# Sums of the queries' squares in the second layer: four-column weights over 512 moving columns, one bank for all pairs, one turn at the end

## The reference, cut to what matters

```python
q = (rms_norm(q_lat, q_a_norm) @ w_uq).reshape(B, S, MLA_HEADS, MLA_QK_DIM)   # 8 heads, 192 = 128 + 64
...
q = rms_norm(q, q_head_norm)          # over the 192 numbers of each token and head
k = rms_norm(k, k_head_norm)
...
q = jnp.concatenate([q[..., :MLA_NOPE_DIM], rope(q[..., MLA_NOPE_DIM:], pos)], axis=-1)
...
o = causal_softmax_attention(q, k, v, 1.0 / math.sqrt(MLA_QK_DIM)).reshape(B, S, MLA_WIDTH)
```

## Time and profile before

| | us |
|---|---|
| median of 3 runs | 1964.53 (1963.85 to 1965.43) |
| the profiled execution | 1966.32, its span 1963.5 |
| TensorE busy | 1875.1, 95% of the span |
| VectorE, ScalarE, GpSimd busy | 966.9, 794.5, 466.8 |
| granted TensorE clock, mean | 0.977 of full |

### The profile page before, as it was taken

One profiled execution on the slowest core, in us unless ns is written; L12 is line 12 of the kernel. 1 busy time (PEld: TensorE's weight loads), 2 busy tenths in 40 slices (PEclk: granted clock), 3 DMA queues, 4 the chain that ended last, 5 costly groups with the idle time before them and its releaser, 6 DMA issues.

```text
span 1963.5 us, 24681 instructions
## 1 busy us (share of the span) xinstructions
PE 1875.1 (95%) x9738; PEld 1481.7 (75%) x9742; DVE 966.9 (49%) x1575; ACT 794.5 (40%) x1401; POOL 466.8 (24%) x471
## 2 busy tenths in 40 slices
PE   6999998999999989999999999999998999999997
PEld 5987776777677756667888888877877788888885
DVE  5345554575446678744433333454555353333334
ACT  4235663444435355554441323233444334232322
POOL 0035541101312124541120201005555202010200
PEclk9999999999999989999999999999999899999999
DMA  4321111221012410001332223221111023223231
GB/s 153 95 78 51 44 43 54 75 86 54 1 53 84 125 54 22 23 23 55 95 98 97 97 86 103 91 86 59 60 54 55 23 85 108 97 94 99 88 100 71
DMA packets 40289, 143.32 MB, mean 73 GB/s; under 512 B 4592, under 2 KB 4976, under 8 KB 40176
## 3 DMA queue, kind: packets, MB, share of 16 engines
q1 hardware_dynamic: 40176, 141.76, 22.5%
HBM read 139.64 MB, written 2.10 MB: 72 GB/s over the span
## 4 chain that ended last, share of the span: by engine, by line
PE 86%; DVE 5%; ACT 4%; POOL 2%; issue 2%; DMA 0%; DVEq 0%; SPq 0%; ACTq 0%; POOLq 0%
PE BANK L273 22%; PE BANK L274 22%; PE BANK L275 22%; PE BANK L854 2%; PE BANK L627 2%; PE BANK L1596 2%; PE BANK L1553 1%; PE BANK L1577 1%; PE BANK L612 1%; PE BANK L911 1%; DVE LH L717 1%; ACT WH L250 1%; PE BANK L2335 1%; PE BANK L2282 1%; PE BANK L2322 1%
## 5 line engine op out<-in xcount | busy, mean ns | idle before, releaser
L250 ACT ACTIVATE WH<-WRAW 128x1024 fp32r<-128x1024 f32 x262 | 273.6, 1046 | 486.6 <-PE BANK L275 449.5
L259 DVE TENSOR_TENSOR WL<-WRAW,WH 128x1024 fp32r<-128x1024 f32 (+1 forms) x249 | 324.8, 1305 | 269.1 <-ACT WH L250 267.6
L273 PE MATMUL BANK<-HH,WH 128*128 128x512 f32 x1048 | 428.5, 409 | 18.6 <-DVE WL L259 18.0
L274 PE MATMUL BANK<-HH,WL 128*128 128x512 f32 x1048 | 411.1, 392 | 0.0
L275 PE MATMUL BANK<-HL,WH 128*128 128x512 f32 x1048 | 410.9, 392 | 0.0
L273 PEld LDWEIGHTS BANK<-HH,WH 128*128 128x128 f32 x1048 | 199.1, 190 | 69.9 <-ACT WH L250 18.7
L274 PEld LDWEIGHTS BANK<-HH,WL 128*128 128x128 f32 x1048 | 198.7, 190 | 44.0 <-issue 5.9
L275 PEld LDWEIGHTS BANK<-HL,WH 128*128 128x128 f32 x1048 | 198.3, 189 | 42.6
L2223 POOL TENSOR_TENSOR HID<-TMP,HID 128x512 fp32r<-128x512 f32 x64 | 83.1, 1299 | 532.9 <-ACT HID L2204 532.9
L273 PE MATMUL BANK<-HID,WH 128*128 128x512 f32 x512 | 203.0, 396 | 0.0
L274 PE MATMUL BANK<-HID,WL 128*128 128x512 f32 x512 | 203.0, 396 | 0.0
(11 more groups left out here) (383 smaller groups left out, 3169.9 us busy)
## 6 DMA issues: line engine op xcount, KB each, us to landing
WRAW<-in_w SPq DMA_DIRECT2D x77, 512.0 KB, 3.5
WRAW<-in_wu SPq DMA_DIRECT2D x64, 512.0 KB, 3.3
WRAW<-in_wd SPq DMA_DIRECT2D x64, 512.0 KB, 3.3
WRAW<-in_w0o SPq DMA_DIRECT2D x8, 512.0 KB, 3.4
WRAW<-in_w1o SPq DMA_DIRECT2D x8, 512.0 KB, 3.5
WRAW<-in_wc SPq DMA_DIRECT2D x8, 512.0 KB, 3.3
WRAW<-in_w2o SPq DMA_DIRECT2D x8, 512.0 KB, 3.4
WRAW<-in_w3o SPq DMA_DIRECT2D x8, 512.0 KB, 3.2
```

What stands on the lines that cost most here:

```text
L250: e.activation(WH[b % NS][:, 0:n], WRAW[b % NR][:, 0:n], ACT.Copy).then_inc(*inc("s_high", ("high", b)))
L259: e.tensor_tensor(WL[b % NS][:, 0:n], WRAW[b % NR][:, 0:n], WH[b % NS][:, 0:n].bitcast(F32), ALU.subtract).then_inc(*inc("s_low_pool" if p ...
L273: e.matmul(dst, ah, bh, start=first and i == 0, stop=False)
L274: e.matmul(dst, al, bh, start=False, stop=False)
```

## The change

It replaces `query_sum`'s twelve matmuls by four. Weights are now four columns cut out of `chosen`, seven columns of which only the fourth is ones, so that pair p adds to row p of the result; the squares are the moving operand, 512 columns. The two heads of a pair go to partitions 0 to 3 and 64 to 67 of bank 7, the rotated halves with 64 rows each (rows 0 to 63 to the first place, 64 to 127 to the second). In the built program the matmuls of L989 of the new kernel have a tile of 128x32 at columns 0 and 64, those of its L991 a tile of 64x32 at (0,0) and (64,64). All four pairs add up in bank 7; the other takes of this stretch go round seven banks (`banks.ring`). Behind pair 3 ScalarE copies the rows of both heads to `m_sums` (128x512, cleared by a new memset on VectorE between gates 0 and 1), and TensorE turns it by four transposes (`query_turn`) behind key sum 7. One pair of activations of 128x32 then makes all factors, in a new order of columns of `QF`.

```diff
-    def take(self, name, *free, of=range(8)):
+    def take(self, name, *free, of=None):
+        of = of or self.ring
...
-            e.memset(either, 0.0).then_inc(*inc("s_const", ("either", 0)))
-            w.wait_ge(*at("either", 0))
-            for b in range(2):
-                e.memset(EPSC[halves[b], 7 + b:8 + b], 1.0).then_inc(*inc("s_const", ("either", 1 + b)))
+            w.wait_ge(*at("const", 3))
+            e.memset(chosen, 0.0).then_inc(*inc("s_const", ("chosen", 0)))
+            w.wait_ge(*at("chosen", 0))
+            e.memset(CF[:, 259:260], 1.0).then_inc(*inc("s_const", ("chosen", 1)))
...
-            w.wait_ge(*at("query factor", un.name // 2))
+            w.wait_ge(*at("query factors"))
...
-                    h, n, i, QF[:, 4 * h + i:4 * h + i + 1], slice(0, 128), len(m_units) % 2,
+                    h, n, i, QF[:, 8 * i + 4 * (h % 2) + h // 2:8 * i + 4 * (h % 2) + h // 2 + 1], slice(0, 128), len(m_units) % 2,
...
             def query_sum(p):
 
-                bank, was = banks.take(("query sum", p), ("query root", p))
+                if p == 0:
+                    _, was = banks.hold("query sums", 7, ("query copied", 1))
+                    for key in was:
+                        w.wait_ge(*at(*key))
+                bank, one = banks["query sums"], chosen[:, 3 - p:7 - p]
+                w.wait_ge(*at("chosen", 1))
+                w.wait_ge(*at("query square", 3 * p + 2))
+                for b in range(2):
+                    e.matmul(bank[64 * b:64 * b + 4, :], one, scr[4 + b], start=p == 0, stop=False, skip_group_check=True)
+                for b in range(2):
+                    made = e.matmul(bank[64 * b:64 * b + 4, :], one[halves[b], :], scr[6][halves[b], :],
+                                    start=False, stop=p == 3, skip_group_check=True)
+                made.then_inc(*inc("s_head_sum", ("query sum", p)))
+
+            def query_turn():
+
+                bank, was = banks.take("query turn", ("query root",))
                 for key in was:
                     w.wait_ge(*at(*key))
-                w.wait_ge(*at("either", 2))
-                w.wait_ge(*at("query square", 3 * p + 2))
-                for b in range(2):
-                    for i in range(NT):
-                        e.matmul(bank[:, 4 * b + i:4 * b + i + 1], scr[4 + b][:, tok[i]], ones[:, 0:1],
-                                 start=(b == 0 and i == 0), stop=False, skip_group_check=True)
+                w.wait_ge(*at("query copied", 1))
                 for i in range(NT):
-                    made = e.matmul(bank[:, i:i + 5:4], scr[6][:, tok[i]], either, start=False, stop=True,
-                                    skip_group_check=True)
-                made.then_inc(*inc("s_head_sum", ("query sum", p)))
+                    made = e.transpose(bank[:, tok[i]], m_sums[:, tok[i]], ident)
+                made.then_inc(*inc("s_head_sum", ("query turn",)))
...
+            banks.ring = range(7)
             queries(0)
...
             key_sum(7)
+            query_turn()
+            banks.ring = range(8)
             gate(7)
...
             gate(0)
+            e.memset(m_sums, 0.0).then_inc(*inc("s_latent_n", ("sums cleared",)))
             gate(1)
...
+            def query_copy():
+                w.wait_ge(*at("query sum", 3))
+                w.wait_ge(*at("sums cleared"))
+                for b in range(2):
+                    c = slice(64 * b, 64 * b + 4)
+                    e.activation(m_sums[c, :], banks["query sums"][c, :], ACT.Copy).then_inc(
+                        *inc("s_head_root", ("query copied", b)))
...
             key_root(6)
-            query_factor(3)
+            query_copy()
             split_high(e, w, after_block("m_g", 6))
             key_root(7)
+            query_factors()
```

More of the change, by code:

```diff
@@ L103, in __init__ @@
     def __init__(self, aps):
-        self.aps, self.i, self.free, self.of = aps, 0, [()] * len(aps), {}
+        self.aps, self.i, self.free, self.of, self.ring = aps, 0, [()] * len(aps), {}, range(8)
     def restart(self):
         self.i, self.free = 0, [()] * len(self.aps)
-    def take(self, name, *free, of=range(8)):
+    def take(self, name, *free, of=None):
+        of = of or self.ring
         j = of[self.i % len(of)]
@@ L158, in program @@
         TMP = sb("TMP", [128, 4, T])
-        EPSC = sb("EPSC", [128, 9])
+        EPSC = sb("EPSC", [128, 7])
         ACC = sb("ACC", [128, T])
@@ L210, in program @@
         ntri, nones = TRI[:, 0:128], TRI[:, 128:256]
-        either = EPSC[:, 7:9]
+        chosen = CF[:, 256:263]
         identb, mnat, mstick, cmask = (CB[:, 128 * i:128 * i + 128] for i in range(4))
@@ L380, in squares_vec, with factor_pe @@
                     *inc("s_acc", ("acc", g, k)))
-        def factor_pe(e, w, g, of=range(8)):
+        def factor_pe(e, w, g, of=None):
             bank, was = banks.take(("sum", g), ("root", g), *[("mean", g)] * (g != "fin"), of=of)
@@ L927, in program @@
         m_raw = [mqn[:, 0, :], mqn[:, 1, :], mqn[:, 2, :], mkpe]
-        cosg = TMP[:, 2, :]
+        cosg, m_sums = TMP[:, 2, :], TMP[:, 0, :]
         m_query = [x for p in range(4) for x in (mqn[:, 2 * p, :], mqn[:, 2 * p + 1, :], mqr[:, p, :])]
@@ L1219, in query_squares, with query_factors @@
                     e.activation(scr[4 + k], m_query[m], ACT.Square).then_inc(*inc("s_square_h", ("query square", m)))
[L1221 to L1228, removed]
+            def query_factors():
+                bank = banks["query turn"].rearrange("p (i b h) -> p i b h", i=NT, b=2)[:, :, :, 0:4]
+                w.wait_ge(*at("query turn"))
+                e.activation(QF[:, :].rearrange("p (i b h) -> p i b h", i=NT, b=2), bank, ACT.Ln, bias=epsq).then_inc(
+                    *inc("s_head_root", ("query root",)))
+                w.wait_ge(*at("query root"))
+                e.activation(QF[:, :], QF[:, :], ACT.Exp, scale=-0.5).then_inc(*inc("s_head_root", ("query factors",)))
+            def query_copy():
[5 more added lines that the diff above has]
+                        *inc("s_head_root", ("query copied", b)))
             def silu(m):
@@ L1247, in l1_scalar @@
             split_high(e, w, after_block("m_q", 1))
-            query_factor(0)
             query_squares(1)
@@ L1255, in l1_scalar @@
             split_high(e, w, after_block("m_q", 2))
-            query_factor(1)
             query_squares(2)
@@ L1262, in l1_scalar @@
             key_squares(7)
-            query_factor(2)
             query_squares(3)
```

## The result

The changed kernel is slower: a median of 1967.40 us (20 runs, 1963.77 to 1971.66) against 1963.98 us for the kernel before (20 runs, 1960.57 to 1967.97). The ratio is 1.0017, with a 95% interval of 1.0010 to 1.0025, so 3.4 us at the middle, 2 to 5 at the ends. That is within 0.2%, but on the other side from the forecast 2.5 us gain, and clear of zero.

What follows compares the result with a forecast made beforehand. TensorE, busy for 95% of the span, was taken as the bound. Terms: -2.7 - 6.4 + 0.45 + 2.9 + 1.7 + 1.6 = -2.5 us, from 1964.5 to 1962.0; range 1957.5 to 1967.5.

Steps and rivals of the forecast that it cites:

- the outcome that had 0.59: Whole kernel: time within 0.2% of the kernel before; faster had 0.26, slower 0.15.
- The groups: Query sums on TensorE: old twelve-matmul groups out, -10.7 us; four new groups of 2.0 in, 8.0; together -2.7.
- The rival that the two row halves don't run side by side: New groups: row halves sharing bank 7 run in turn, 0.86 longer per group, +3.4, 1965.4 us; chance 0.12.
- The clock behind the groups: Half-clock stretches behind the four old groups: no fall expected with the new ones, 12.9 us take half, -6.4.
- The rival that the clock falls as before: Behind the new groups: half clock stays, the 6.4 not given back, +4.4 in all, 1968.9 us; chance 0.13.
- The turn and the attention's wait: Four transposes behind key sum 7, +0.45 us; first scores wait for VectorE's sixth copy of value tiles, +1.6.
- The first query tile: First query tile takes key tile 7's bank and waits for ScalarE's last key copy: +2.9 us, ends 2.3 and 3.1.
- What this idle does to the clock: Behind the idle at the first query tile: one clock fall, 3.4 us at half, +1.7; ends 0 and 1.7.
- Nothing elsewhere: Behind the attention: TensorE stays the chain, so nothing else should absorb the gain; no term in the sum.

Runs made afterwards that it cites:

- values: Kernel before, old sums kept, with only the tiles of values in the changed kernel's banks (3 to 7, 0 to 2): 1972.61 us, ratio 1.0048.
- later banks: Changed kernel with every layer behind the attention back in the banks of the kernel before: 1968.49 us, ratio 1.0023.
- idle filled: Changed kernel with two fp32 matmuls of 512 columns, result unread, in TensorE's idle time ahead of the first scores: 1960.66 us, ratio 0.9989.
- query bank: Changed kernel with the first query tiles in banks 4, 5, 6, 0, so the first follows key tile 0 again: 1966.10 us, ratio 1.0007.
- kernel before with the new banks: Kernel before, old sums kept, with only the tiles of values in the changed kernel's banks: 1972.61 us, ratio 1.0048.
- the kernel with both corrections: Changed kernel with first query tiles in banks 4, 5, 6, 0 and tiles of values in 6, 7, 0 to 5: 1956.29 us, ratio 0.9967.

## Why the prediction was wrong, step by step

The forecast was -2.5 us; the places up to 555 add up to +3.3, and the medians differ by 3.4. The measured time lies just inside the range, at its upper end, and the change is under 0.2%, the outcome that had 0.59. The sign is not the forecast one. That the time still lies inside is luck: the +1.7 for a fall that did not come, and a gain that the sum did not have, stood against the losses that it lacked.

*The groups*, 2.0 each: right, 1.91 each, -3.1 for the four instead of -2.7. The rival that the two row halves don't run side by side is ruled out: L991 took 0.95 for both halves, which write one bank on partitions 0 to 3 and 64 to 67. The Trainium skill, "TensorEngine Tiling (Array Packing)", "Gotcha 1: PSUM Pressure", says that different row tiles cannot access the same PSUM bank simultaneously; for outputs on such different partitions this trace disagrees.

*The clock behind the groups*, -6.4: right in kind, no fall behind any of the four, in any profile with the new groups, and one behind each in both with the old. The rival that the clock falls as before is ruled out. In size it was -5.8: the stretch gained 8.97, of which the groups are 3.13. I had halved the time at half clock. A matmul of a tile took 0.427 from start to start at half clock (six from 449.39 to 451.95 in the kernel before) and 0.231 at full (eleven from 452.28 to 454.82); some of these rows:

```profile
449.82 0.63 PE L273 MATMUL BANK<-HH,WH 128*128 128x512 f32 x1
450.24 0.63 PE L274 MATMUL BANK<-HH,WL 128*128 128x512 f32 x1
...
452.28 0.40 PE L273 MATMUL BANK<-HH,WH 128*128 128x512 f32 x1
452.52 0.40 PE L274 MATMUL BANK<-HH,WL 128*128 128x512 f32 x1
```

So 3.4 us at half clock cost 1.56, not 1.7. The Trainium skill, "TensorE: Matmul & The Clock Gate", "Terms", gives the penalty as the time at the lower clock times what the clock lacks, one half; these rows give 0.46 of the time.

*The turn and the attention's wait*, 0.45 + 1.6: right, 2.09 together.

*The first query tile*, +2.9: right in its cause, 2.55 in size. ScalarE's last two key copies end at 395.18 and the tile starts at 395.40. The memset, which I put at 0.45, cost nothing: VectorE's split behind it took 1.22 in the changed kernel's profile and 1.73 in the one before, and ScalarE waited 3.13 for the first key copy, against 3.15. VectorE and ScalarE after, then VectorE before:

```profile
388.44 0.48 DVE L1123 MEMSET TMP<- 128x512 f32 x1
389.39 1.22 DVE L261 TENSOR_TENSOR WL<-WRAW,WH 128x1024 fp32r<-128x1024 f32 x1
...
392.58 0.63 ACT L1217 ACTIVATE SCR<-mkn 128x512 f32<-128x512 f32 x1 [3.13 <-DVE mkn L1128]
...
394.11 1.07 ACT L1211 ACTIVATE mkn<-BANK 128x512 f32<-128x512 f32 x2
```

```profile
392.26 1.73 DVE L259 TENSOR_TENSOR WL<-WRAW,WH 128x1024 fp32r<-128x1024 f32 x1
```

*What this idle does to the clock*, +1.7: wrong. The idle of 2.4 stands in four of the profiles (the changed kernel, values, later banks, idle filled), and full clock in front of and behind it in all four. The row that I took it from says less than I read in it: the idle time of 1.75 ahead of L612 is in all ten profiles, with half clock behind it in four and full clock in six.

*The step that failed* is the one that is not there: the clock behind the second idle time. I asked the question of the 2.9 us at the query tile and not of the 1.6 us at the scores, where the answer was +6.4: the clock fell in all four profiles that have this idle with nothing in it and in none of the six that don't. Why it falls there and not at the query tile is not shown. One difference is what stands around the gap: at the query tile matmuls of 512 columns on both sides, behind the gap at the scores matmuls of 128 columns and then 256. That alone does not decide it, since an idle time of 1.5 further on has matmuls of 128 columns behind it too, and all ten profiles keep full clock there. The kernel before:

```profile
867.64 1.23 PE L1577 MATMUL BANK<-CF,SCR 128*128 128x128 f32 x8 [1.49 <-POOL SCR L2114]
```

*Nothing elsewhere* ("behind the attention TensorE stays the chain, so nothing else should absorb it"): wrong by +1.2 at the output product, and by 0.6 and 1.1 at the two places further on. I had followed the moved banks up to the attention and stopped there.

*A gain that the sum did not have.* The change also narrows `EPSC`, a small tile of constants, from nine columns to seven, so that everything laid out behind it in SBUF begins elsewhere. In each of the eight kernels with seven columns the weight products that read a tile behind `EPSC` (`OG...`, `HID`, `eog`, `mq...`, `mk...`) follow each other 0.0013 us faster on average than in the two with nine, 0.2330 for 0.2342, while those that read `HH` and `HL`, which lie ahead of it, take 0.2276 in all ten. Before and after, the first and last of 384 in a row:

```profile
1205.86 0.40 PE L273 MATMUL BANK<-HID,WH 128*128 128x512 f32 x1
...
1295.59 0.40 PE L275 MATMUL BANK<-HID,WH 128*128 128x512 f32 x1
```

```profile
1206.59 0.40 PE L275 MATMUL BANK<-HID,WH 128*128 128x512 f32 x1
...
1295.95 0.40 PE L277 MATMUL BANK<-HID,WH 128*128 128x512 f32 x1
```

That is 89.73 us before and 89.36 after. There are 2424 such matmuls in the program, so some 3 us in all, about what the moved later banks cost. No run changes the width alone, so that the address is the cause is argued and not shown.

Together, up to 555: 6.4 + 1.2 - 1.7 - 0.35 + 0.6 - 0.4 is 5.75 us, the distance between -2.5 and +3.3.

## What to carry to other kernels

Where banks are handed out in turn, an edit that takes one more or one fewer moves every later bank and with it whom each first tile waits for: follow the phase to the end of the program, or restore it, as a few added numbers did here for some 12 us. Do not price an idle time of TensorE by its length alone: 1.5 us ahead of the scores cost 8, while 2.4 us ahead of the query tile cost 2.5, and the idle time of 1.75 in the first layer had half clock behind it in four profiles of ten. And compare two profiles place by place by the starts of the same matmuls, since one execution's total may carry falls of the clock that have nothing to do with the edit.

## What the runs showed that I had not expected

The half-clock stretch in the attention lasted 13.7, 20.5, 13.7 and 17.1 us (changed kernel, query bank, later banks, kernel before with the new banks), though TensorE was busy throughout; work at half clock did not end it at once. What ends it, and why its length differs, no run here settles. It would account for the wide scatter of the kernels that have it: the query-bank kernel's runs go from 1956.39 to 1968.64, those of the kernel with both corrections from 1954.83 to 1957.40. The former fall into two groups, four at 1956.39 to 1961.02 and eight at 1965.53 to 1968.64, as if in a third of them the clock had held. The granted clock of each run fits that: 0.979 to 0.982 in the four, 0.974 to 0.977 in the eight, and the distance of the two means, 0.0049 of 1965 us, is what 19 us at half clock make. The one with a profile is of the upper group, so where the clock held in the four is not shown.

Two matmuls that compute nothing, put into an idle time of about their own length, made a kernel 5.5 to 6.7 us faster.
